# Neighbour attention with heads stacked over all 128 rows and its sums once per pair; steps of the stick-breaking stage in another order

## The reference

```
def stick_breaking_attention(q, k, v):          # 8 heads, blocks of 128 queries
    z = einsum('bqhd,bshd->bhqs', qb, k) * scale
    log_keep = where(mask, log_sigmoid(-z), 0.0)
    after = cumsum(log_keep, axis=3, reverse=True) - log_keep
    a = where(mask, exp(log_sigmoid(z) + after), 0.0)
    return einsum('bhqs,bshd->bqhd', a, v)

def neighborhood_attention(q, k, v, k_ctx, v_ctx, rpb):   # 8 heads, 8 x 64 grid
    s_loc = q . k over a window of 8 x 16 tokens, * scale + bias   # masked elsewhere
    s_ctx = q . k_ctx over 256 context tokens, * scale
    p = softmax(concatenate([s_loc, s_ctx]))
    return p[window] @ v + p[context] @ v_ctx
```

## Time and profile before

| what | us |
|---|---|
| median of 3 runs | 3125.72 |
| range of these runs | 3122.38 to 3125.88 |
| the profiled execution, own time | 3128.8 |
| its span, first to last instruction | 3127.3 |
| stick-breaking stage, first scores to last sums | 228 to 345 |
| neighbour stage, its slots | 1434.8 to 1577.7 |

### The profile page before, as it was taken

How to read it: one execution, slowest core, us unless ns; L and a number is a source line. 1 busy time by engine, 2 the same in 40 slices (tenths; PEclk the granted TensorE clock), 3 DMA queues, 4 the chain that set the end, 5 groups by cost and what they waited for, 6 DMA issues and landing times. The chain is left out here.

```text
span 3127.3 us, 43142 instructions
## 1 busy us (share of the span) xinstructions
PE 3005.6 (96%) x16088; PEld 2615.5 (84%) x16088; DVE 2262.9 (72%) x4392; ACT 1336.6 (43%) x2344; POOL 802.7 (26%) x696
## 2 busy tenths in 40 slices
PE   7998899999999999988999989999999999999998
PEld 5667688887777888866778868999999999999998
DVE  4768586774885867743453368978788888988886
ACT  3667532234664322333442233349843333343333
POOL 1000100001001200042000124668734435434431
PEclk9999999999999999989999989999999999999999
DMA  3001244433222443321123223655599999999993
GB/s 144 25 29 54 66 165 146 132 108 105 88 88 95 161 143 133 100 69 50 44 71 102 94 81 102 188 191 217 230 369 329 326 356 327 344 329 322 338 340 116
DMA packets 189710, 525.33 MB, mean 168 GB/s; under 512 B 15792, under 2 KB 80176, under 8 KB 187200
## 3 DMA queue, kind: packets, MB, share of 16 engines
q1 hardware_dynamic: 130432, 308.84, 29.0%
q0 software_dynamic: 45104, 164.68, 14.8%
q10 hardware_dynamic: 13968, 49.06, 4.1%
HBM read 484.22 MB, written 38.31 MB: 167 GB/s over the span
## 5 line engine op out<-in xcount | busy, mean ns | idle before, releaser
L239 PE MATMUL bank<-h_hi,w_hi 128*128 128x512 f32 (+1 forms) x2528 | 963.2, 381 | 39.4 <-DVE h_lo L325 12.8
L239 PE MATMUL bank<-h_lo,w_hi 128*128 128x512 f32 (+1 forms) x2528 | 944.7, 374 | 0.0
L213 DVE TENSOR_TENSOR w_lo<-w_raw,w_hi 128x1024 fp32r<-128x1024 f32 (+1 forms) x452 | 579.7, 1283 | 274.4 <-ACT w_hi L207 271.3
L207 ACT ACTIVATE w_hi<-w_raw 128x1024 fp32r<-128x1024 f32 (+1 forms) x508 | 544.9, 1073 | 481.3 <-PE bank L239 461.5
L239 PE MATMUL bank<-h_hi,w_lo 128*128 128x512 f32 (+1 forms) x2528 | 591.5, 371 | 0.1
L239 PEld LDWEIGHTS bank<-h_hi,w_hi 128*128 128x128 f32 x2528 | 482.8, 191 | 123.9 <-issue 25.8
L239 PEld LDWEIGHTS bank<-h_lo,w_hi 128*128 128x128 f32 x2528 | 483.5, 191 | 57.9 <-issue 2.2
L239 PEld LDWEIGHTS bank<-h_hi,w_lo 128*128 128x128 f32 x2528 | 459.5, 189 | 61.9 <-issue 4.6
L239 PE MATMUL bank<-e_hi,w_hi 128*128 128x384 f32 x1024 | 345.8, 338 | 1.4 <-DVE x L2629 1.1
L239 PE MATMUL bank<-e_lo,w_hi 128*128 128x384 f32 x1024 | 344.5, 336 | 0.0
L2450 POOL DMA_INDIRECT own_row<-in_u_rows,own_e x128 | 166.1, 1298 | 261.4 <-DVE sums L2585 207.5
(11 more groups left out here) (441 smaller groups left out, 4461.8 us busy)
## 6 DMA issues: line engine op xcount, KB each, us to landing
w_raw<-in_w SPq DMA_DIRECT2D x476, 512.0 KB, 3.9
ada_w<-in_ada_w POOLq DMA_DIRECT2D x48, 512.0 KB, 3.6
expert_weights<-G ACTq DMA_DIRECT2D x12, 2048.0 KB, 7.2
Gin<-expert_weights SPq DMA_DIRECT2D x32, 768.0 KB, 10.5
w_raw<-in_w SPq DMA_DIRECT2D x32, 704.0 KB, 4.1
hidden_ahead<-u_stage ACTq DMA_DIRECT2D x56, 192.0 KB, 4.0
ahead<-hidden_ahead SPq DMA_DIRECT2D x28, 384.0 KB, 9.1
fx_crow<-fox_cum POOLq DMA_DIRECT2D x8, 512.0 KB, 4.0
```

The costliest lines, as they stand in the source:

```text
L207: sc.activation(w_hi[s][:, 0:n], w_raw[raw_slot[u]][:, 0:n], ACT.Copy).then_inc(*w_hi_made.next(u))
L213: ve.tensor_tensor(w_lo[s][:, 0:n], w_raw[raw_slot[u]][:, 0:n], w_hi[s][:, 0:n], ALU.subtract).then_inc(*w_lo_made.next(u))
L239: m = te.matmul(out, wt, moving, start=(not low and k == 0 and moving is hi), stop=(low and k == len(blocks) - 1))
```

## The change

Neighbour stage. The query's high and low part now each fill 128 rows (twice the same 64 channels), and a key's high part stands above its low part, so that two fp32r matmuls per score block (L1840, L1841 of the changed kernel) with a contraction of 128 rows replace one float32 matmul of 64 rows. ACT makes the high parts (`query_high`, 4 instructions of 64x512; `key_high`, 2 of 64x896), DVE the low ones (`query_low`, 4; `key_low`, 2). From pair 1 on the weights come in the order k, q, v. The probabilities of all four tiles of a pair are kept (PT, in part in a buffer of the context that is free by then), ACT copies each head's four turned blocks in two instructions of 128x256 instead of one of 128x512, and the sums of a pair are made at once in slot 0 of the next (`sums_of`, 14 matmuls of 128 to 512 columns). The turning of v moves from before a pair's first scores to the middle of its slot 0, behind the scores. In pairs 1 and 2 three chunks of the next pair's k unit stand before the first scores. `less` is one buffer instead of two; POOL refills each third as soon as it was last read. Some buffers are shared with other stages' (qf, kf, vT).

Stick-breaking stage. PE takes two chunks of the next pair ahead of the first scores of pairs 1 and 2, and DVE takes the first of a slot's two pieces before the scan instead of after the additions.

```diff
 stick, tensor() and vector()
@@
                     a, b, c = (2, 2, 2) if p < 3 else (1, 1, 0)
+                    if 0 < p < 3:
+                        run(more, 2)
@@
                         ve.tensor_scalar(low[hh][m % 2][:, 0:kw], z[hh][m % 2][:, 0:kw], -1.0, 0.0, ALU.mult, ALU.min).then_inc(*dve.next("sb low", hh, m))
+                run(more, 1)
                 if 1 <= m <= steps:
@@
-                run(more, 2 if i < TT - 1 else 1 << 30)
+                run(more, 1 if i < TT - 1 else 1 << 30)
 neighbour, PE
@@
+                if name == "k" and p:
+                    te.wait_ge(*act.at("na ctx", "v", p - 1))
+                if name == "v":
+                    te.wait_ge(*act.at("na ctx", "k", p))
@@
-                chunk = 4 if p < 3 else 2
+                    a, b = (4, 3) if p < 3 else (2, 1)
+                    if 0 < p < 3:
+                        run(more, 3)
...
+                        if i == 0:
+                            te.wait_ge(*dve.at("na", "k lo", p))
+                            te.wait_ge(*dve.at("na", "q lo", p))
...
-                        te.matmul(s_bank[hh][:, 0:NA_BAND], lhs, k[p % 2][rows, i * P:i * P + NA_BAND], start=True, stop=True)
-                        te.matmul(s_bank[hh][:, NA_BAND:T], lhs, k[p % 2][rows, NA_CTX:], start=True, stop=True).then_inc(*pe.next("na scores", hh, m))
-                run(more, chunk)
+                        for to, keys in ((slice(0, NA_BAND), slice(i * P, i * P + NA_BAND)), (slice(NA_BAND, T), slice(NA_CTX, NA_CTX + CTX))):
+                            te.matmul(s_bank[hh][:, to], q_hi[p % 2][:, hh, tile], k[p % 2][:, hh, keys], start=True, stop=False)
+                            t = te.matmul(s_bank[hh][:, to], q_lo[p % 2][:, hh, tile], k[p % 2][:, hh, keys], start=False, stop=True)
+                        t.then_inc(*pe.next("na scores", hh, m))
+                run(more, a)
...
-                    for j, block in enumerate((i2, i2 + 1, 5, 6)):
+                run(more, b)
+                if m < steps and i == 0:
+                    turn_all(p, m - 1 if m else None)
+                if m and i == 0:
+                    run(more, 2)
+                    sums_of(p - 1)
 neighbour, ACT's list for the next pair
@@
+        def pair_scalar_ctx(p):
+            take_bias(p)
+            yield
+            split_hi(U[p][0] + 1)
+            yield
+            yield
+            split_hi(U[p][1] + 1)
+            copied(p, "k", kf)
+            yield
+            key_high(p)
+            yield
+            copied(p, "q", qf, -SCALE)
+            query_high(p)
+            yield
+            split_hi(U[p][2] + 1)
+            yield
+            copied(p, "v", vT)
 neighbour, DVE's list
@@
+            split_lo(U[p][1] + 1)
+            yield
+            yield
+            key_low(p)
+            yield
+            query_low(p)
+            yield
+            split_lo(U[p][2] + 1)
 neighbour, POOL
@@
-                if p >= 2:
-                    gp.wait_ge(*dve.at("na least", 1, 4 * (p - 1) - 1))
-                for edge in range(3):
+                for edge, used in enumerate((0, 2, 3)):
+                    if p:
+                        gp.wait_ge(*dve.at("na least", 1, 4 * (p - 1) + used))
 weights of pairs 1 to 3
@@
-    u8 += [units_of(pair(w[:, 512 * n:512 * (n + 1)], p)) for p in range(4) for n in range(3)]
+    u8 += [units_of(pair(w[:, 512 * n:512 * (n + 1)], p)) for p in range(4) for n in ((1, 0, 2) if p else (0, 1, 2))]
```

More of the change, by code:

```diff
@@ L1668, in by_row, with role, unit_of @@
             return columns.rearrange("p (c r) -> p r c", c=DH)
+        def role(p, n):
+            return "qkv"[n] if p == 0 else "kqv"[n]
+        def unit_of(p, name):
+            return U[p][[role(p, n) for n in range(3)].index(name)]
         def pair_tensor_ctx(p):
             for n in range(3):
[L1672 to L1677, removed]
@@ L1714, in pair_vector_ctx, with copied @@
-        def pair_vector_ctx(p):
-            for n in range(3):
-                yield
-                if p or n:
-                    split_lo(U[p][n] + 1)
-                yield
+                yield from unit(u, [(lin[u % 2][:, :], h_blocks)] + ([(xb, hc_blocks)] if name != "q" else []), ready)
+        def copied(p, name, dst, scale=1.0):
+            u = unit_of(p, name)
+            sc.wait_ge(*w_used.at(u))
+            if name == "k" and p:
+                sc.wait_ge(*pe.at("na v turned", p - 1))
+            if name == "v":
+                sc.wait_ge(*dve.at("na", "k lo", p))
+            if name == "q" and p:
+                sc.wait_ge(*dve.at("na", "q lo", p - 1))
+            sc.activation(dst[:, local if name != "q" else slice(0, T)].rearrange("p (c r) -> p c r", c=DH), by_column(lin[u % 2][:, :]), ACT.Copy,
+                          scale=scale).then_inc(*act.next("na", name, p))
+            if name != "q":
+                at = 0 if name == "k" else CTX
+                sc.activation(dst[:, NA_CTX:], x_bank[:, at:at + CTX], ACT.Copy).then_inc(*act.next("na ctx", name, p))
+            if name != "v":
+                bank_of.taken(u, act)
@@ new lines, in key_high, with key_low @@
+        def key_high(p):
+            sc.wait_ge(*act.at("na ctx", "k", p))
+            if p == 0:
+                sc.wait_ge(*pool.at("na edges"))
+            for hh in range(2):
+                rows = head_rows(hh)
+                sc.activation(k[p % 2][rows, hh, :], kf[rows, :], ACT.Copy).then_inc(*act.next("na", "k hi", p))
+        def key_low(p):
+            ve.wait_ge(*act.at("na", "k hi", p))
+            for hh in range(2):
+                rows = head_rows(hh)
+                ve.tensor_tensor(k[p % 2][beside(hh), hh, :], kf[rows, :], k[p % 2][rows, hh, :], ALU.subtract).then_inc(*dve.next("na", "k lo", p))
@@ new lines, in sums_of @@
+        def sums_of(p):
+            for hh in range(2):
+                te.wait_ge(*act.at("na moved", hh, 4 * p + TT - 1))
+            te.wait_ge(*act.at("na v natural", p))
+            if p:
+                te.wait_ge(*dve.at("na out", p - 1))
+            for block in (5, 0, 1, 2, 3, 4, 6):
+                a, b, at = (0, TT, 8 + 4 * (block - 5)) if block > 4 else (max(0, block - 1), min(TT, block + 1), max(0, 2 * block - 1))
+                for hh in range(2):
+                    rows = head_rows(hh)
+                    t = te.matmul(o_bank[rows, a * P:b * P], v[p % 2][:, block, rows], PT[hh][:, at:at + b - a, :], start=(block == 5), stop=(block == 6))
+                    if block == 6:
+                        t.then_inc(*pe.next("na sums", hh, p))
```

161 lines of the change are left out of this document (89 added, 72 removed).

## The result

| | before | after |
|---|---|---|
| median of 20 runs each, us | 3125.47 | 3130.32 |
| profiled execution, own time | 3128.8 | 3127.02 |
| its span | 3127.3 | 3125.6 |
| neighbour stage, from PE's last projection of pair 0 | 145.4 | 150.1 |
| stick-breaking stage, from its first scores | 117.8 | 116.8 |

A forecast was written before the change was run, and what follows sets the result against it. PE, 96% busy, was taken to set the end. Neighbour stage plus 3.4 us, stick-breaking minus 0.8, gave 2.6 on 3128.8, so 3131.4; 3.1 lower for the runs' median, 3128.3, rounded to 3128.5; 8-of-10 range 3117 to 3139.

The forecast's parts named there:

- The sum for the neighbour stage: Neighbour stage laid out in time with work, waits and clock, ending at 1581.0 against 1577.65: plus 3.4 us.
- What ends last at a pair's change: Neighbour stage: PE waits at starts of pairs 1 to 3 for ACT's and DVE's queues, 2.0, 5.3 and 5.4 us.
- PE's own work: Neighbour stage: stacked scores save 3.7 us and sums once per pair 3.3 us, together 7.0.
- the two prices: Neighbour stage, PE: scores at 0.94 us a slot instead of 1.17, sums at 3.7 us a pair instead of 4.5.
- The timetable: Neighbour stage, PE's work and waits pair by pair: from about 1432.2 to 1581.0.
- The clock: Neighbour stage: low clock behind the long waits costs PE 2.2 us at each of pairs 2 and 3, none at pair 1.
- rival 2: Slower, 3138: clock falls at pairs 1, 2, 3 and behind the last probabilities, 13.6 instead of 4.4 us; chance 0.34.
- POOL beside the query's low part: Neighbour stage: POOL's third part of `less` slows DVE's low query by 0.6 us, 1.1 if they collide whole.
- The stick-breaking stage: Pairs go from 30.9 to 29.7 us twice, less 0.6 for DVE and 1.0 in the last pair: minus 0.8 us.
- Rival 3: The stick-breaking order does nothing, since DVE is its bound: 3129.3; chance 0.48 together with the forecast.
- A sign that was badly chosen: Neighbour pair starts less than 37 us apart would show that ACT or DVE was not the chain laid out.

The follow-up runs named there:

- e1: Kernel before with only the stick-breaking edits (two chunks ahead of first scores, one DVE piece ahead of the scan); ratio 1.0000 of before.
- e3: Changed kernel, but k and v units wait for ACT's copy of the context part only ahead of their context matmuls; ratio 0.9999 of before.
- e5: Changed kernel, but in neighbour slots 1 to 3 ACT's copies of turned probabilities go behind its exponentials and a piece of the next pair's list; 0.9958 of before.
- e7: e6 with the last neighbour pair's projection chunks dealt thinner, leaving 4 for the last softmax; ratio 0.9938 of before.
- e12: Changed kernel with only the last neighbour pair's chunks dealt thinner (3 per slot, 4 kept for the last softmax); ratio 1.0001 of before.
- e4: Changed kernel with ACT's key and query high parts made sooner, the query's ahead of slot 2's exponentials, and DVE's low parts likewise; ratio 1.0020 of before.
- e2: Changed kernel with the stick-breaking edits undone, so the neighbour stage's change alone; ratio 1.0021 of before.
- e8: e7 with the change's two stick-breaking edits undone; ratio 0.9939 of before.
- e11: Kernel before, with ACT's exponentials ahead of the copies of turned probabilities in neighbour slots 1 to 3; ratio 1.0013 of before.
- e6: e5 and e3 together, with ACT's pieces moved into the gaps and DVE's key parts one piece sooner; ratio 0.9943 of before.
- e9: e7 with DVE's low parts of weights and outputs one slot later in the stick-breaking stage, and ACT's high part sooner; ratio 0.9934 of before.
- e10: e9 with DVE making the neighbour stage's query low part ahead of slot 3's least; ratio 0.9935 of before.

## Why the prediction was right, and by how much it was off

The direction and the mechanism were right: PE's saved work is there, and the waits for ACT's and DVE's queues at a pair's change eat more than all of it. The size was not: 2.6 us forecast, about 5.6 measured.

**The sum for the neighbour stage**: 3.4 forecast, 4.7 measured (150.1 against 145.4). That it came so near is in part luck. Of the 148.8 us laid out, 19.0 were waits and 4.4 clock; of the 150.1 measured, 16.3 and 7.4. The waits were taken 2.7 too long and the clock's cost 3.0 too small, and the two errors all but cancel; PE's own work was 1.0 more than laid out. The base is luck too: against e1's 142.7 us for the same stage of before it would be 7.4 measured. The first scores of pairs 1 to 3 were laid out 33.8, 74.4 (the wait's end and three chunks) and 115.2 us after pair 0's projections; they came at 33.5, 75.5 (the chunks ran at low clock) and 114.8.

**What ends last at a pair's change**: right. Waits of 2.0, 5.3 and 5.4 were forecast, 1.4, 4.9 and 5.5 came, for the named instructions. ACT's queue from the transposes of slot 2 to the copy of v took 12.0 us (1485.27 to 1497.24) where 12.5 were laid out. In slot 1 1.2 was forecast and 0.7 came, at the end 2.7 and 1.2 against 2.3 and 0.8. In all 19.0 forecast, 16.3 measured. e3 and e5 show that the waits are the cause: they went with their mechanism, and the time with them.

**PE's own work**: 7.0 saved by the two prices, but before's 134.3 (above) less e7's busy 125.5 is 8.8. The timetable, which counted the matmuls, had it: 148.8 less 19.0 and 4.4 is 125.4. That it stood 1.9 below 134.3 less 7.0 went unnoticed.

**The clock**: the term that was mis-sized. 4.4 us forecast, 7.4 measured: 6.8 us less the 1.3 that lie in the wait, halved, is 2.8 at pair 2; 1.6 at pair 3; and (6.8 - 0.8) / 2 = 3.0 at the end, where I had counted none though I had forecast a wait of 2.7 there. e12 takes the end's share away, with its waits. So rival 2's mechanism came true at three places of its four, though not at pair 1.

**POOL beside the query's low part**: the four took 3.79 us (the row below), and 2.83 in e4, where POOL did not run: 1.0, not the 0.6 taken.

```profile
1494.04 3.79 DVE L1723 TENSOR_TENSOR na_qlo<-norm_y,na_qhi 64x512 fp32r<-64x512 f32 x4
```

By the Trainium skill ("SBUF — State Buffer", Who interferes with whom) a DVE instruction with two SBUF inputs contends with a GpSimd one that reads SBUF. The trace agrees: 1.0 of the 1.1 us that the prediction had for a whole collision came. POOL's instruction stretched too, to 2.18 us beside e4's key parts (two in 3.18, where they take 2.20 in the changed kernel), from 1.27 alone. POOL of e4:

```profile
1488.50 2.18 POOL L1950 TENSOR_TENSOR na_less<-na_mask,na_bias 128x512 f32<-128x512 f32 x1 [13.35 <-DVE na_small L1923]
1501.54 1.27 POOL L1950 TENSOR_TENSOR na_less<-na_mask,na_bias 128x512 f32<-128x512 f32 x1 [10.85 <-DVE na_small L1923]
```

**The stick-breaking stage**: -0.8 forecast, -1.0 in the two profiles, -0.6 in e1. Pairs 1 and 2 lasted 29.2 and 30.8 us for 29.7 twice, the wait for the low query was 0.4 at pair 2, the new ones for w_hi 1.8. Neither difference can be put down to the edits, since the stage's length also goes with its clock. Before's order took 117.8 us in before and in e2 (23.9 us at clock 0.50), 117.1 in e8 (20.5) and 115.7 in e11 (10.2); the edited order 117.3 in e3 (17.1) and e4 (13.7), 117.2 in e1 (13.7), 116.8 in after (10.2) and 116.0 in e5, e6, e7 and e12 (3.4). At the same 10.2 us of low clock the edited order was even 1.1 us longer (116.8 against 115.7). Rival 3, that it does nothing, fits best: e1 and e8 show no difference in the runs.

**A sign that was badly chosen.** Starts of a neighbour pair less than 37 us apart were to show that the chain is another. Pairs 0 and 1 started 33.5 us apart (1425.83 and 1459.28), so by this sign the prediction would be wrong. But its own timetable has 33.8 there, since the sums of pair 0 now stand in pair 1: the sign contradicts the sum it was to test. The next two pairs started 42.0 and 39.3 us apart, and the waits named are what shows the chain.

**What stays open.** The stages give 4.7 less 1.0, 3.7 us, at the lower edge of what the runs say (3.7 to 7.5). With e1's 142.7 for before's neighbour stage they would give 7.4 less 1.0, 6.4 us, so the 5.6 of the runs lies between what two executions of before's neighbour stage give, which differ in one low stretch. Of the changed form's stage there are two executions too, 150.1 and 150.4 (e2). The changed kernel's times go with the clock in the same way: executions with a mean clock of 0.981 took 3126.5 to 3127.7 us, those with 0.977 to 0.979 3130.9 to 3134.4; the profiled one is of the first sort, while before's, at 0.979, is among the long ones of before. How often each stretch comes is not known, since only profiled executions show it, and so the 5.6 us can't be divided further.

## What to carry to other kernels

Before pricing a new wait, look whether the engine that is waited for stands idle ahead of it: here ACT stood 4 us at a time for one input (51.8 us in 13 waits), in the slot shown with another ready behind it, and moving the copies behind the work that could go first was worth 18 us of the stage, more than all that the change itself saved. Work that is moved ahead "into the gap" must be followed round the loop through every queue (e4). A wait's price includes the low clock behind it, at the end of a stage as well. And one profiled execution is no fixed base: the same stage with the same waits took 145.4 and 142.7 us.

## What the runs showed of the hardware

- PE's clock in the neighbour stage fell to 0.50 behind a wait of 1.9 us (e4) and behind every one of 2.3 and more (after, e2, e3, e4, e11, e12), and not behind those of 1.75 (e11, twice), 1.6 (e5) and 1.4 (after). Behind the same wait of 2.03 us it fell in before and did not in e1. In e5, e6 and e7 it stayed at 1.00 for the whole stage.
- In the stick-breaking stage, where PE waits anyway, low clock costs only part of what it costs a PE that is never idle. Before's order took 115.7 us with 10.2 us at clock 0.50 (e11) and 117.8 with 23.9 (before): 13.7 us more at half speed cost 2.1 us, where an engine with no idle time would lose 6.8 (an estimate, half of 13.7). The edited order took 116.0 with 3.4 (e7) and 116.8 with 10.2 (after). e9 and e10, which have the same instructions there, took 113.5 with 3.4 and 115.0 with 10.2.
- Two executions of the same instructions ahead of the change differed by 6.5 us, at a mean clock of 0.95 and 0.98, more than the whole effect of the change.
- DVE and POOL stretched each other: four DVE subtractions of 64x512 took 3.79 us beside a POOL one (after) and 2.83 alone (e4), the POOL one of 128x512 1.65 (after) and 2.18 (e4) for 1.27.
